# Two transformer blocks on one core: the forgetting heads' gate projection with its operands exchanged and the result turned on VectorE

## The reference

```
z = hn @ w_in[l]                        # hn: 256 x 1024, the normed and modulated tokens
...
qd = _rms_norm(z[..., FOX_Q0:FOX_K0].reshape(B, S, FOX_HEADS, HEAD_DIM), fox_qk_g[l, 0])
kd = _rms_norm(z[..., FOX_K0:FOX_V0].reshape(B, S, FOX_HEADS, HEAD_DIM), fox_qk_g[l, 1])
vd = z[..., FOX_V0:FOX_F0].reshape(B, S, FOX_HEADS, HEAD_DIM)
log_f = jax.nn.log_sigmoid((z[..., FOX_F0:IN_COLS] + fox_fb[l]).astype(jnp.float32))
o_d = _forgetting_attention(qd, kd, vd, log_f)
```

## Time and profile before

| what | value |
|---|---|
| median of 3 runs | 2172.9 us (2172.66 to 2175.04) |
| the profiled execution's own time | 2172.73 us |
| its span, first to last instruction | 2170.8 us |
| PE busy | 2077.2 us, 96% |
| DVE busy | 1416.7 us, 65% |
| ACT busy | 1109.7 us, 51% |
| mean granted TensorE clock | 0.972 |

### The profile page before, as it was taken

The page is one execution under the profiler, slowest core; times in us unless marked ns, Lnnn a source line. Parts: engine busy times, 40 slices in busy tenths (PEclk is TensorE's granted clock), DMA queues, the critical chain, the costliest instruction groups (busy, mean ns, idle before and its releaser), DMA issues.

```text
span 2170.8 us, 33092 instructions
## 1 busy us (share of the span) xinstructions
PE 2077.2 (96%) x13748; PEld 1859.7 (86%) x13748; DVE 1416.7 (65%) x1874; ACT 1109.7 (51%) x1757; POOL 60.6 (3%) x40
## 2 busy tenths in 40 slices
PE   8999899999999999999999999899999999989999
PEld 7798788888988888887999887699989998868998
DVE  5467568887556748988755766655576556666555
ACT  6348535445337725445554544555555555355544
POOL 0110000000110000000001000000000100000000
PEclk9999999999999999999999997899999999889999
DMA  7353278996444248996555432255545553214553
GB/s 270 117 194 116 69 271 316 390 382 219 139 175 136 98 145 321 387 382 276 191 175 178 153 123 75 76 175 189 182 166 188 178 182 136 78 59 146 184 181 130
DMA packets 56164, 409.55 MB, mean 189 GB/s; under 512 B 6608, under 2 KB 6992, under 8 KB 7888
## 3 DMA queue, kind: packets, MB, share of 16 engines
q1 hardware_dynamic: 46512, 330.23, 42.9%
q10 hardware_dynamic: 9504, 77.21, 8.9%
HBM read 406.37 MB, written 1.05 MB: 188 GB/s over the span
## 4 chain that ended last, share of the span: by engine, by line
PE 84%; DVE 8%; ACT 6%; issue 2%; DMA 1%; POOL 0%; DVEq 0%; ACTq 0%; SPq 0%; POOLq 0%
PE bank L555 24%; PE bank L556 24%; PE bank L557 24%; PE bank L974 4%; DVE weights_low L388 1%; PE bank L1720 1%; ACT weights_high L377 1%; PE bank L907 1%; PE bank L919 1%; DVE work L1332 1%; ACT work L435 1%; DVE work L513 1%; ACT weights_high L378 1%; ACT work L436 1%; ACT scratch L452 1%
## 5 line engine op out<-in xcount | busy, mean ns | idle before, releaser
L388 DVE TENSOR_TENSOR weights_low<-raw_weights,weights_high 128x1024 fp32r<-128x1024 f32 x584 | 700.1, 1240 | 418.7 <-ACT weights_high L377 416.4
L555 PE MATMUL bank<-h_high,weights_high 128*128 128x256 f32 x2944 | 851.8, 289 | 20.0 <-DVE h_low L524 12.9
L556 PE MATMUL bank<-h_low,weights_high 128*128 128x256 f32 x2944 | 839.5, 285 | 0.0
L557 PE MATMUL bank<-h_high,weights_low 128*128 128x256 f32 x2944 | 839.3, 285 | 0.0
L377 ACT ACTIVATE weights_high<-raw_weights 128x1024 fp32r<-128x1024 f32 x292 | 309.1, 1058 | 690.9 <-PE bank L557 643.0
L555 PEld LDWEIGHTS bank<-h_high,weights_high 128*128 128x128 f32 x2944 | 571.3, 194 | 40.4 <-DVE work L513 14.1
L556 PEld LDWEIGHTS bank<-h_low,weights_high 128*128 128x128 f32 x2944 | 571.6, 194 | 3.7 <-issue 1.9
L557 PEld LDWEIGHTS bank<-h_high,weights_low 128*128 128x128 f32 x2944 | 571.3, 194 | 0.0
L378 ACT ACTIVATE weights_high<-raw_weights 128x1024 fp32r<-128x1024 f32 x292 | 305.1, 1045 | 0.0
L555 PE MATMUL bank<-weights_high,hidden_high 128*128 128x512 f32 x608 | 237.6, 391 | 1.8 <-DVE weights_low L388 1.8
L556 PE MATMUL bank<-weights_low,hidden_high 128*128 128x512 f32 x608 | 237.4, 390 | 0.0
(11 more groups left out here) (274 smaller groups left out, 1947.6 us busy)
## 6 DMA issues: line engine op xcount, KB each, us to landing
raw_weights<-in_stream SPq DMA_DIRECT2D x310, 1024.0 KB, 4.9
work<-in_ada ACTq DMA_DIRECT2D x64, 1152.0 KB, 10.2
consts<-in_consts SPq DMA_DIRECT2D x1, 2048.0 KB, 12.6
work<-in_row ACTq DMA_DIRECT2D x2, 836.0 KB, 6.2
x<-in_x SPq DMA_DIRECT2D x1, 1024.0 KB, 5.0
out_x<-x SPq DMA_DIRECT2D x4, 256.0 KB, 2.0
gain_row<-in_final SPq DMA_DIRECT2D x1, 512.0 KB, 13.2
vec<-in_vec SPq DMA_DIRECT2D x1, 169.0 KB, 12.5
```

The costliest lines, as they stand in the source:

```text
L388: dve.tensor_tensor(low[:, c], raw[:, c], high[:, c].bitcast(F32), ALU.subtract).then_inc(m.raw_done[plan.index[name] % RAW], 1)
L555: pe.matmul(out, aH, bH, start=start, stop=False, skip_group_check=True)
L556: pe.matmul(out, aH, bL, start=False, stop=False, skip_group_check=True)
L557: return pe.matmul(out, aL, bH, start=False, stop=stop, skip_group_check=True)
```

## The change

The four gate columns become the stationary operand and h streams past, all 256 tokens at once. The 128 stationary columns are four groups of 32, and each group begins with the four gate columns, the other 28 being zero; the host lays the chunk out so. The result is feature-major: in each group of 32 partitions of the bank the first four rows are the gates of all 256 tokens. DVE transposes 32 x 32 blocks: group g of partitions takes tokens 32g to 32g + 31 of both token tiles, so four transposes of 32 partitions x 64 elements give the gates token-major in `temp(m)`, after which DVE waits for its own write (`step`) and the addition of the bias reads every token tile's four columns there.

```diff
-            for tt in range(2):
-                for kt in range(KT):
-                    t = slice(kt * T + tt * P, kt * T + tt * P + P)
-                    c = slice(kt * 256, kt * 256 + 4)
-                    mm = three(pe, b[:, tt * 4:tt * 4 + 4], m.hH[:, t], m.hL[:, t], wH[:, c], wL[:, c], kt == 0, kt == KT - 1)
+            for kt in range(KT):
+                t = slice(kt * T, (kt + 1) * T)
+                c = slice(kt * 256, kt * 256 + P)
+                mm = three(pe, b[:, 0:T], wH[:, c], wL[:, c], m.hH[:, t], m.hL[:, t], kt == 0, kt == KT - 1)
             done(name, mm)
...
             full("ff")
-            dve.tensor_tensor(cols(m, FOX_Y, 8), m.bank(plan, "ff")[:, 0:8], rows(m, "fb"), ALU.add).then_inc(V, 1)
+            turned = temp(m)[:, 0:64]
+            for g in range(4):
+                r = slice(32 * g, 32 * g + 32)
+                ins = dve.transpose(tiles(turned[r], 2), tiles(m.bank(plan, "ff")[r, 0:T], 2)[:, :, r])
+            step(ins)
+            dve.tensor_tensor(tiles(cols(m, FOX_Y, 8), 2), tiles(turned, 2)[:, :, 0:4], tiles(rows(m, "fb"), 2), ALU.add).then_inc(V, 1)
...
-            np.concatenate([w[:, 2560:2564], np.zeros((D, 252), np.float32)], 1), 8)
+            np.concatenate([w[:, 2560:2564], np.zeros((D, 28), np.float32)] * 4 + [np.zeros((D, P), np.float32)], 1), 8)
```

## The result

The changed kernel takes 2150.57 us (median of 4 runs, 2149.95 to 2151.55) against 2172.78 in the same comparison: a ratio of 0.990, 95% interval 0.9887 to 0.9913. Two more sets of runs gave 2148.79 and 2149.35 us. The profiled execution took 2151.06 us, its span is 2149.0.

A forecast was written before the change was run, and what follows sets the result against it. PE alone was taken to set the time from `cx1` to task 4's scores, mostly at half clock. A gain of 9.6 us per layer, 19.2 for both, from 2172.73 gave 2153.5 us, range 2149.5 to 2160.

The forecast's parts named there:

- ff: Gate projection on PE: 24 wide matmuls take 2.97 us in place of 7.91, a gain of 4.94 us.
- sfq and sfk: PE's pieces right behind `ff`: at full clock 1.85 us in place of 3.69, a gain of 1.84 us.
- Task 4: PE's work between `sfk` and `gv`: 1.55 us at full clock in place of 2.55, a gain of 1.00 us.
- gv: PE's work after task 4: 5.94 us at full clock in place of 7.81, a gain of 1.87 us.
- PE's lead at task 5: After `gv`, PE runs 9.65 us ahead of the kernel before.
- t: Time DVE's four transposes and their wait add before the bias addition: 0.7 us, bounds 0.3 to 1.9.
- DVE would be the bound at task 5: At task 5 DVE is ready 0.6 us later than PE, so the maxima there come 9.1 us earlier.
- The wait at gs0: PE's 4.78 us wait at `gs0` for the layer norm on DVE and ACT stays about as long.
- how the later half-clock stretches fall: Later half-clock stretches, meeting the shifted work differently, may add or take some 2 us over both layers.
- The clock that falls anyway: Rival: four columns are not the cause, the clock still falls after `ff`; layer gains 4.94 us, 2162.8 us; chance 0.09.
- The dear transpose: Rival: costly 32-partition transposes out of PSUM make DVE the bound; 2176.1 us at 3 us each; chance 0.02.
- given back: Rival: the 9.6 us lead is lost before the layer ends, time about 2172.7 us; chance 0.03.

The follow-up runs named there:

- the mixed one: Kernel before the change, with its 48 four-column matmuls of `ff` issued between the 14 taps of `cx1`; 2156.56 us, ratio 0.9923.
- The moved split: Changed kernel with its transposes moved before task 4's maxima and the first output-projection chunk's split moved from task 6 to task 8; 2151.06 us, ratio 0.9898.

## Why the prediction was right

**What bounds it, and the clock.** PE set the time from `cx1` to task 4, and the narrow matmuls were what brought the clock down. The prediction rested on the place of the fall alone, inside `ff` in both layers; the run with 256 columns and the mixed one show it. The prediction did not split its gain between the two things that changed; the run with 256 columns does: of 9.4 us a layer, 6.9 come with the width and 2.5 with the count.

**The terms, first layer.** *ff*: 3.05 us where 2.97 was given. *sfq and sfk*: 1.81 for 1.85. *Task 4*: 1305.84 to 1307.30, 1.46 for 1.55. *gv*: 5.94 as said. PE's lead at task 5 is 9.74 us (23.41 from `ff` to task 5 before, 13.67 now), predicted 9.65.

**The transposes.** Here a term was too small: t = 1.06 us, not 0.7. I had put each at 0.14 us from start to start, by adding the elements' price to the spacing of two one-element copies. They stand 0.26 apart, which is nearly the 0.244 us that one of them lasts; they hardly overlap, unlike the copies. The value was inside the bounds (0.3 to 1.9). The figure of the Trainium skill ("VectorE: DVE Perf Modes", The three transpose paths), 311 ns for a transpose of 128x128 bf16, gave the estimate t = 1.24, nearer than my own. By the sum, 10.32 - 1.06 = 9.26 us a layer; 9.40 were measured at `gs0`. Of the rest 0.09 is that `gv` began 7.87 us earlier against the start of `ff`, not 7.78. That DVE would be the bound at task 5 held, and twelve transposes confirmed it. One subtraction in that paragraph is off by 0.1 us (L2149 at 1312.9, not 1313.0), and nothing hangs on it.

**The wait at gs0** stayed, 5.11 us for 4.78, as the prediction said, and the clock falls there as before.

**What the sum did not hold.** It gave 19.2 us; the two stretches hold 18.8, and the medians 22.2, 23.6 and 22.8 in the three comparisons. The prediction put some 2 us on how the later half-clock stretches fall, with either sign. This term was too small: 3.4 to 4.8 us more than the stretches, and the first median already lies below the forecast's own range of 2151 to 2157.5. That the range held is in part luck. In the traces the time from the second `gs0` to the end of the last matmul is 247.3 and 247.3 us for the kernel before, and 246.2, 244.7 and 244.8 for the changed one; between the first `gs0` and the second `ff` it is 519.3 and 519.2 against 515.9, 518.4 and 519.5. One place is the start of the second feed-forward, 10.16 us from its first matmul. Before, in the first layer and in the second:

```profile
1405.44:1415.60 10.16, 10.16 (x61) 10.00 (x62) 6.22 (x13) 4.59 (x8) 1.28 (x1) 0.70 0.27 86
...
1975.29:1985.45 10.16, 10.16 (x61) 10.00 (x62) 6.14 (x13) 4.51 (x8) 1.21 (x1) 0.69 0.27 89
```

And in the changed kernel:

```profile
1397.34:1407.50 10.16, 9.62 (x78) 9.42 (x79) 8.23 (x14) 6.55 (x11) 1.90 (x1) 1.00 0.26 85
...
1954.08:1964.24 10.16, 9.63 (x66) 9.42 (x66) 6.72 (x13) 5.10 (x8) 1.79 (x1) 0.83 0.28 92
```

The code there is the same; the clock is 1.00 and 0.83 in place of 0.70 and 0.69, and 78 and 66 matmuls are done in place of 61. The second trace of the kernel before has 0.71 and 0.69, the other two of the changed one 0.83 and 1.00, then 0.69 and 1.00. So much of the surplus sits in these later stretches, and in five of six cases they are kinder to the changed kernel. Another part is chance of a single trace: the first `ff`, ahead of which the two kernels do the same, begins at 1299.53 and 1298.03 us in the traces of the kernel before and at 1300.98, 1297.16 and 1297.52 in those of the changed one. The surplus came in all three comparisons, so it is more than the noise of a median. The other kernels show it less (medians less stretches: 2.2 us with 256 columns, 1.5 spread out, 1.0 with twelve transposes, -0.8 with half the narrow matmuls), which would fit a dependence on where the later work comes to lie; but this is argued, not shown, for no run moved the later work alone.

**The rivals.** The clock that falls anyway is refuted by the 256-column run. The Trainium skill's rule ("TensorE: Matmul & The Clock Gate", Part 1), that the clock follows how busy PE has been, was weighed on its side. The traces differ from it if busy is read as the busy column of the profile: with 64 columns that column is full at 0.50 as at 1.00. The dear transpose is out (0.26 us each, not 2.6). Nothing was given back in the changed kernel but the 0.3 us that the transposes cost: from `gs0` to the output projection it takes 25.90 us as before. The moved split shows what giving back looks like.

## What to carry to other kernels

Where a small projection stands in a row of its own, look at the granted clock inside it and behind it: here 4.9 us of 9.4 were lost in the work behind it. Let the long side stream and the short side be stationary, or deal the narrow matmuls out between wide ones; both kept the clock through the stretch in the traces but for one fall in `gv`, and the second needs no new layout. Before adding work to the engine that follows, find its longest wait nearby: the transposes fit into 6 us of waiting and were placed where there was none.

## What the runs showed of the hardware

A full busy column does not mean that the clock holds: PE was busy 7.64 of 7.64 us in a stretch with a granted clock of 0.70, with 64 streamed columns. The distance between starts gives no sign either: 0.111 us with four columns and with 64, where the clock fell, and 0.124 with 256, where it held.

The damage outlasts its cause. Behind `ff`, the products of `sfq`, `sfk` and task 4 kept PE busy 7.10 of 7.69 us and the clock did not return; it came back in `gv`, in the first layer 4.2 us after its start. Yet behind 24 narrow matmuls the clock fell in `sfq` and was back in task 4 (0.57, then 0.91), so what brings it back is not settled here.

With the cause removed, falls remain that come in one execution and not in the next: in `gv` in one of six layers of the changed kernel, in `gv` of one layer with the transposes moved, in `gu` of one with twelve. An experiment on such a kernel is best read by its stretches, where two executions agree within 0.02 us if the clock falls alike in them (and differ by 1.17 where it did not), before its total, where they differ by 5 us and more (2156.33 to 2161.37 with 256 columns, 2162.99 to 2175.13 in ten runs of the kernel before).
